# Two-expert MoE: expert results meet in a half-sum array and are scattered to the outputs, in place of an array by tokens read back at the end

## The chip, the cores and the metric

One Trainium2 chip, one core. The metric is the device time of one launch in microseconds; a comparison is made on the same chip, kernel against kernel. A core has TensorE (PE), VectorE (DVE), ScalarE (ACT), GpSimd (POOL) and SyncE (SP), and 16 DMA engines that all queues share.

## The reference

A layer of attention and retention on 512 prompt frames and 64 sample frames (576 tokens of 1024 float32 values), then a mixture of experts over 32 experts. The change touches only the second half, and in it how the experts' results reach the outputs:

```python
def hier_moe(hn, w_group, w_expert, w_gate, w_up, w_down):
    t = hn.reshape(-1, d)
    pg = softmax(t @ w_group);  g_sel = argmax(pg);  p_sel = pg[g_sel]
    el_sel = (t @ w_expert).reshape(-1, N_GROUPS, EXPERTS_PER_GROUP)[g_sel]
    top_p, top_i = top_k(softmax(el_sel), 2)
    w = p_sel * top_p / sum(top_p)
    eid = g_sel * EXPERTS_PER_GROUP + top_i        # two experts, of one group
    for e in range(32):
        a = silu(t @ w_gate[e]) * (t @ w_up[e])
        out = out + comb[:, e] * (a @ w_down[e])
...
x = x + hier_moe(rmsnorm(x, norm2_g), ...)
```

N_GROUPS is 4, EXPERTS_PER_GROUP is 8, an expert has 256 hidden units. Both experts of a token lie in one group of eight. Every token is computed by two experts, so 1152 rows in all.

## The kernel before, in words

The first part (projections, attention, retention, output projection, router logits) runs by a list of steps that `plan()` writes; it isn't touched but for one place: SP writes zeros over `y_d`, a DRAM array with two rows of 1024 for each token, by nine 512 KB transfers (line 744).

**The pairs.** The 32 experts are taken two at a time, as 16 pairs. A pair holds up to 64 rows of each of its two experts in the 128 partitions. Its weights are 6 MB (gate, up and down of two experts, 1 MB each), which SP streams from DRAM into a ring of 18 units of 1 MB, three pairs ahead at most (lines 786 to 809). For pair p:

- POOL gathers the tokens' hidden rows from `hn_d` into a row buffer `xg(p)` by an indirect transfer (`gather`, line 920). There are five row buffers (`XROWS`), so `gather(p)` waits for the scatter of pair p-5; it also waits for PE's transposes of pair p-4.
- PE transposes them (line 1272), DVE scales them into `xgT` (line 2174), PE does gate and up (line 1278), ACT the sigmoid (line 1680), DVE the product (lines 2211, 2214), PE transposes it (line 1286), DVE copies it (line 2228) and PE does down (line 1293).
- DVE adds: `ride` (line 2248) writes over the row buffer either hidden row plus y, where this is the token's first expert (flag 1 in `rides`), or y alone. POOL scatters the buffer to `y_d` (`scatter`, line 930): first expert's rows to the lower half, second expert's to the upper.

A row of the 128 that holds no token has an index beyond the bound, and nothing is moved for it. POOL runs its queue in program order:

```python
for p in range(LAST - 1):
    if p + 4 < NPAIR:
        gather(p + 4)
    scatter(p)
```

So `gather(p + 4)` waits until the scatter of pair p-1 has landed, and `scatter(p)` stands behind that. PE runs ahead: transposes of pair p+1, activation transposes of p-1, gate and up of p, down of p-1. Down of a pair waits for DVE's sum of the pair before (the same PSUM banks).

**The end.** The last two pairs (14, 15) aren't scattered. Their results are split in a high and a low half (ACT line 1691, DVE line 2281) and put on the tokens' rows by one-hot matmuls (`oh_last`, `last_rows`, lines 1334 and 1335). When the scatters of pairs 0 to 13 have landed, SP reads `y_d` back, two rows for each token (line 831, ten transfers), DVE and POOL add the two (lines 2289, 975), DVE adds the one-hot sums (line 2338), and SP stores the outputs (lines 838, 840).

More than 64 rows of one expert would run a further loop (`LEVELS`); with these inputs no expert has so many and the loop isn't entered, before or after.

Of the kernel before, what the change touches and what calls it, by code (L numbers as in the profile page):

```python
# [14 lines left out]
P = 128  # L15
# [23 lines left out]
FIN_UNIT, OVER_UNIT, YTOK_UNIT, OH_UNIT = 12, 6, 6, 4  # L39
LAST = NPAIR - 1  # L40
YOUT = [16 * (NPAIR // 2 - 1)] * 2
FIN_BANKS = [4, 0, 6, 2, 4]
# [3 lines left out]
PER_LEVEL = 7  # L46
# [3 lines left out]
FAR = 2047.0  # L50

# [183 lines left out]

def constants():
# [37 lines left out]

    dest = np.stack([np.stack([tok, tok + T_TOK * k], -1) for k in range(2)], 1) - FAR
    put("dest", dest)
    put("pair_row1", np.tile(np.arange(NE) % 2 * CAP + 1, (P, 1)))
# [25 lines left out]
def stream_step(nc, consts, x_prompt, x_sample, cache_ret_state, cache_swa_k, cache_swa_v,  # L303
# [11 lines left out]
    y_d = nc.dram_tensor("y_d", [2 * T_TOK, D], F32, kind="Internal").ap()  # L315
# [9 lines left out]
    with ExitStack() as ctx:  # L325
# [122 lines left out]
        with nc.sbuf_tensor("units_ahead_oh", [P, OH_UNIT, KD * FF], F32):  # L448
            with nc.sbuf_tensor("oh_last", [P, 2, NT, P], F32R) as oh_last:
                pass  # L450
        w_moe_a = sb("w_moe_a", [P, UNITS_A, KD * FF])

        with nc.sbuf_tensor("units_ahead", [P, FIN_UNIT - UNITS_A, KD * FF], F32):
            with nc.sbuf_tensor("y_last", [P, 2, 2, D], F32R) as y_last:
                pass
# [22 lines left out]
        rides, rides_l = ssq_qk[:, 0:NPAIR], ssq_qk[:, NPAIR:2 * NPAIR]  # L478

# [17 lines left out]
        pair_wr = const("cos").rearrange("p (j c) -> p j c", c=2 * NPAIR)  # L497
        rank_k, row_k, row_l = small[:, 60:70], small[:, 70:80], small[:, 80:90]
        lvl_a, lvl_b, level0 = small[:, 130:140], small[:, 140:150], small[:, 150:151]
        pair_dst = sb("pair_dst", [P, 2 * NT, 2 * NPAIR], F32R)  # L500
        wr_k = sb("wr_k", [P, 2, NT, 2])
        idx = sb("idx", [P, 2 * NPAIR], I32)
        idx_now = sb("idx_now", [P, 2, 1], I32)
        wr = sb("wr", [P, 2, NPAIR])
        wr_now = sb("wr_now", [P, 2, 1])
        ride_now = sb("ride_now", [P, 1])
# [5 lines left out]

        def y_tok(t, k):
            n = 2 * t + k
            return units(YTOK_UNIT + n // 2, 1)[:, 0, n % 2 * D:n % 2 * D + D]
# [105 lines left out]
        y_out = [sem(f"y_out{u}") for u in range(2)]  # L621

# [13 lines left out]
        L_out = sem("L_out")  # L636
        L_step = sem("L_step")
# [15 lines left out]
        yl_hi = sem("yl_hi")  # L653
        yl_lo = sem("yl_lo")
        oh_fin = sem("oh_fin")
        fin_ps = sem("fin_ps")
        fin_out = sem("fin_out")
# [46 lines left out]
        def _(sp):  # L704
# [8 lines left out]
            def load_gu_of(p, e):  # L713
                for m, v in enumerate((gate_v, up_v)):
                    sp.dma_start(units(gu_at(p, e, m), 1)[:, 0, :], v[2 * p + e]).then_inc(gu_in[p % 4], 16)  # L715
# [5 lines left out]
            def load_dn(p):  # L721
                for e in range(2):
                    sp.dma_start(dn_at(p, e), down_v[2 * p + e]).then_inc(dn_in[p % 4], 16)  # L723
# [46 lines left out]
            sp.dma_start(units(gu_unit(3, 0), 1)[:, 0, :], gate_v[6]).then_inc(gu_in[3], 16)  # L770
            sp.wait_ge(half_used, OUT1)
            sp.dma_start(units(gu_unit(2, 1) + 1, 1)[:, 0, :], up_v[5]).then_inc(gu_in[2], 16)
            sp.dma_start(dn_at(2, 0), down_v[4]).then_inc(dn_in[2], 16)
            sp.dma_start(units(gu_unit(3, 0) + 1, 1)[:, 0, :], up_v[6]).then_inc(gu_in[3], 16)
            sp.wait_ge(acc_done, NJ)
            load_gu_of(2, 0)
            sp.dma_start(units(gu_unit(2, 1), 1)[:, 0, :], gate_v[5]).then_inc(gu_in[2], 16)
            sp.dma_start(dn_at(2, 1), down_v[5]).then_inc(dn_in[2], 16)
# [21 lines left out]
            for half, landed in enumerate((first_half, gu_in[LAST % 4])):  # L800
                ks = slice(half * 4 * FF, half * 4 * FF + 4 * FF)
                for e in range(2):
                    for m, v in enumerate((gate_v, up_v)):
                        sp.dma_start(units(gu_unit(LAST, e) + m, 1)[:, 0, ks], v[2 * LAST + e][:, ks]
                                     ).then_inc(landed, 16)
            sp.wait_ge(y_ps, LAST - 2)
            load_dn(LAST)

            sp.wait_ge(slots_ready, 1)
            n_most = sp.value_load(most_i[0:1, 0:1], min_val=0, max_val=T_TOK)  # L810
            with sp.If(n_most > CAP):
                sp.wait_ge(y_ps, NPAIR)
                with sp.Fori(1, LEVELS) as lv:
                    with sp.Fori(0, NPAIR) as p:
                        it = (lv - 1) * NPAIR + p

                        sp.wait_ge(L_y, it + 1)
                        for e in range(2):
                            for m, v in enumerate((gate_v, up_v, down_v)):
                                sp.dma_start(units(OVER_UNIT + (2 * e + m if m < 2 else 4 + e), 1)[:, 0, :],  # L820
                                             v[bass.ds(p * 2 + e, 1)].rearrange("o p n -> p (o n)")
                                             ).then_inc(L_w, 16)
                sp.wait_ge(L_done, NPAIR * (LEVELS - 1) + 1)

            for u in range(2):
                sp.wait_ge(y_out[u], YOUT[u])
            for t in range(NT):
                n = out_rows(t)
                for k in range(2):
# [1561 lines left out]
```

## Time and profile before

| | us |
|---|---|
| three runs | 564.68, 568.24, 569.65 |
| median of the runs | 568.24 |
| span of the profiled execution, first to last instruction | 563.3 |
| MoE: first pair's matmuls to the last instruction | 323 to 563.3 |
| read back of `y_d` begins (SP line 831) | 535.5 |
| last pair's down matmuls end (PE line 1322) | 546.4 |
| TensorE's mean granted clock, 1 being full | 0.953 |

The profiled execution's time outside its span isn't listed by itself; the median of the runs is 4.9 us above the span, the lowest 1.4 us. In the rows below, a time stands from the span's start. A DMA's landing is counted from the start of the instruction that issues it.

### The profile page before, as it was taken

The page shows a single profiled execution, that of the slowest core. Times are in us where ns is not written, and L with a number is a line of the kernel's source. Part 1 is how long each engine was busy: PE and PEld are TensorE (multiplying, and loading weights), DVE is VectorE, ACT ScalarE, POOL GpSimd, SP SyncE. Part 2 cuts the span into 40 slices and gives each one's busy share as a digit, 9 for nine tenths or more (in the row PEclk, how much of TensorE's full clock was granted, in tenths as well). Part 3 has the DMA queues.
Part 4 walks back from the last instruction along what each step waited for, and adds up shares of the span by engine and source line. Part 5 has one row for each costly group of instructions (what it writes and reads, how often), then busy time and mean ns, then how long its engine had stood idle before and what let it go on. Part 6 is the DMA issues. An engine that isn't in the chain of part 4 may idle for free.

```text
span 563.3 us, 7848 instructions
## 1 busy us (share of the span) xinstructions
PE 501.6 (89%) x2907; PEld 318.3 (57%) x2907; DVE 262.0 (47%) x593; ACT 131.4 (23%) x351; POOL 156.9 (28%) x279
## 2 busy tenths in 40 slices
PE   4976999899999999999994799979999869778984
PEld 4955877777777777778884654333333333333333
DVE  2859588767344565672226622322334221112535
ACT  4754343354546322232111100000000000000110
POOL 5446683042214554741104300211111220100003
PEclk9989999799999999999997699979999998889998
DMA  8440220040026832219949799999999999999997
GB/s 294 158 127 3 75 76 2 1 144 8 2 74 234 240 123 86 79 52 407 420 167 351 296 385 396 417 423 417 417 421 420 418 420 417 419 420 423 411 411 225
DMA packets 35031, 144.75 MB, mean 257 GB/s; under 512 B 5842, under 2 KB 8994, under 8 KB 23216
## 3 DMA queue, kind: packets, MB, share of 16 engines
q1 hardware_dynamic: 26320, 129.94, 58.8%
q0 software_dynamic: 4528, 9.01, 4.3%
q10 hardware_dynamic: 4144, 5.28, 2.9%
q8 instruction: 24, 0.39, 0.3%
q14 instruction: 15, 0.12, 0.1%
HBM read 138.16 MB, written 17.30 MB: 276 GB/s over the span
## 4 chain that ended last, share of the span: by engine, by line
PE 46%; DMA 18%; DVE 13%; SPq 10%; issue 4%; ACT 3%; POOL 1%; DVEq 0%; POOLq 0%; ACTq 0%
PE banks L1051 19%; SPq L715 7%; PE banks L1278 6%; DMA w_moe_b<-in_w_up_dram 5%; DMA y_d<-rows,idx 3%; DMA y_d<-y_sb,idx 3%; SPq L723 3%; DMA w_moe_b<-y_d 3%; PE banks L1109 3%; DMA y_d<-x_row,idx 2%; PE banks L1293 2%; PE banks L1045 2%; DMA y_sb<-hn_d,idx 2%; PE banks L1194 1%; PE banks L1189 1%
## 5 line engine op out<-in xcount | busy, mean ns | idle before, releaser
L872 POOL TENSOR_TENSOR w_lo<-w_raw,w_hi 128x512 fp32r<-128x512 f32 x52 | 70.6, 1371 | 119.6 <-ACT w_hi L1556 117.7
L1278 PE MATMUL banks<-w_moe_b,xgT 128*64 128x512 f32 x224 | 67.8, 626 | 9.6 <-DMA w_moe_b<-in_w_up_dram 6.6
L1278 PE MATMUL banks<-w_moe_a,xgT 128*64 128x512 f32 x224 | 69.0, 639 | 4.9 <-DMA w_moe_a<-in_w_up_dram 4.9
L2211 DVE SCALAR_TENSOR_TENSOR glu_b<-banks,wr,glu_a 128x256 f32<-128x256 f32 x15 | 7.2, 483 | 98.4 <-ACT glu_a L1680 98.4
L1680 ACT ACTIVATE glu_a<-banks,wr 128x256 f32<-128x256 f32 x15 | 7.1, 475 | 196.6 <-PE banks L1278 183.5
L1051 PE MATMUL banks<-w_hi,xT_hi_a 128*128 128x512 f32 (+3 forms) x124 | 50.5, 408 | 1.6 <-DVE xT_lo_a L1742 1.6
L1278 PEld LDWEIGHTS banks<-w_moe_b,xgT 128*64 128x64 f32 x224 | 21.1, 144 | 48.7 <-issue 45.7
L1051 PE MATMUL banks<-w_lo,xT_hi_a 128*128 128x512 f32 (+3 forms) x124 | 48.2, 388 | 0.0
L1051 PE MATMUL banks<-w_hi,xT_lo_a 128*128 128x512 f32 (+3 forms) x124 | 48.0, 387 | 0.0
L1278 PEld LDWEIGHTS banks<-w_moe_a,xgT 128*64 128x64 f32 x224 | 21.7, 146 | 27.6 <-issue 25.8
L1051 PE MATMUL banks<-w_hi,xT_hi_b 128*128 128x512 f32 (+3 forms) x92 | 35.7, 388 | 0.8 <-issue 0.8
L1051 PE MATMUL banks<-w_lo,xT_hi_b 128*128 128x512 f32 (+3 forms) x92 | 34.0, 370 | 0.0
L1051 PE MATMUL banks<-w_hi,xT_lo_b 128*128 128x512 f32 (+3 forms) x92 | 33.9, 368 | 0.0
L1556 ACT CAST w_hi<-w_raw 128x512 fp32r<-128x512 f32 x52 | 30.7, 613 | 12.0 <-DMA w_raw<-in_w_out_dram 10.5
L1293 PE MATMUL banks<-w_moe_a,actT 128*64 128x512 f32 x144 | 32.6, 593 | 0.5 <-DVE actT L2228 0.5
L1600 ACT ACTIVATE probs<-banks,soft,rstd_qk 128x208 f32<-128x208 f32 (+1 forms) x40 | 20.6, 519 | 51.0 <-DVE soft L1922 51.0
L1051 PEld LDWEIGHTS banks<-w_hi,xT_hi_a 128*128 128x128 f32 (+1 forms) x124 | 23.8, 192 | 6.8 <-ACT xT_hi_b L1498 1.8
L1051 PEld LDWEIGHTS banks<-w_hi,xT_lo_a 128*128 128x128 f32 (+1 forms) x124 | 23.8, 192 | 5.0
L1051 PEld LDWEIGHTS banks<-w_lo,xT_hi_a 128*128 128x128 f32 (+1 forms) x124 | 23.8, 192 | 3.8
L920 POOL DMA_INDIRECT rows<-hn_d,idx x7 | 7.2, 1031 | 55.9 <-DMA y_d<-rows,idx 45.3
L2174 DVE TENSOR_TENSOR xgT<-banks,g_both 128x1024 f32<-128x1024 f32 x15 | 18.3, 1219 | 8.8 <-PE banks L1272 8.8
L1293 PEld LDWEIGHTS banks<-w_moe_a,actT 128*64 128x64 f32 x144 | 11.0, 137 | 19.9 <-issue 19.2
(334 smaller groups left out, 934.2 us busy)
## 6 DMA issues: line engine op xcount, KB each, us to landing
w_moe_a<-in_w_down_dram SPq DMA_DIRECT2D x20, 1024.0 KB, 20.3
w_moe_a<-in_w_gate_dram SPq DMA_DIRECT2D x16, 1024.0 KB, 11.6
w_moe_a<-in_w_up_dram SPq DMA_DIRECT2D x16, 1024.0 KB, 13.9
w_moe_b<-in_w_gate_dram SPq DMA_DIRECT2D x14, 1024.0 KB, 17.1
w_moe_b<-in_w_up_dram SPq DMA_DIRECT2D x14, 1024.0 KB, 17.0
w_moe_b<-in_w_down_dram SPq DMA_DIRECT2D x10, 1024.0 KB, 25.8
w_raw<-in_w_in_dram SPq DMA_DIRECT2D x34, 256.0 KB, 4.1
y_d<-in_consts_dram SPq DMA_DIRECT2D x9, 512.0 KB, 10.8
```

The source lines that it names most:

```text
L715: sp.dma_start(units(gu_at(p, e, m), 1)[:, 0, :], v[2 * p + e]).then_inc(gu_in[p % 4], 16)
L723: sp.dma_start(dn_at(p, e), down_v[2 * p + e]).then_inc(dn_in[p % 4], 16)
L872: nc.gpsimd.tensor_tensor(w_lo[:, s, :], w_raw[:, s, :], w_hi[:, s, :].bitcast(F32), ALU.subtract).then_inc(split, 1)
L920: pool.indirect_dma_start(out=xg(p), out_offset=None, in_=hn_d, in_offset=bass.IndirectOffsetOnAxis(ap=idx[:, p:p + 1], axis=0), bounds_ch ...
L1045: l = mm(into, a_hi[:, P * t:P * t + P], w, start=(kk == 0 and q == 0), stop=(kk == KD - 1 and q == 1))
L1051: l = mm(into[0:R, 0:width], a, w, start=(kk == 0 and q == 0), stop=(kk == KD - 1 and q == 2))
L1109: l = mm(sideA[64 * c2:64 * c2 + 64, b, 256 * hl + dst:256 * hl + dst + n], sqT[gs, ORDER.index(t) % DEEP, 2 * hh + hl, CH * c2:CH * c2 + CH],
L1278: l = mm(acc[64 * e:64 * e + 64, u, :].rearrange("p (m f) -> p m f", m=2), xgT[:, xu, k, 64 * e:64 * e + 64], units(at_e[e], 2)[:, :, k * ...
L1293: l = mm(acc[64 * e:64 * e + 64, 2 + n, :], actT[:, j, 64 * e:64 * e + 64], mats[e][:, j * D + n * 512:j * D + n * 512 + 512], start=(j == ...
L1556: nc.scalar.copy(w_hi[:, s, :], w_raw[:, s, :]).then_inc(hi_done, 1)
L1600: af(probs[0:R, q, hl, :], sideA[0:R, b, 256 * hl:256 * hl + KEYS], ACT.Exp, scale=rstd_qk[0:R, h + hl:h + hl + 1], bias=soft[0:R, q, 2 + ...
L2174: tt(xgT[:, u], at[:, 0:2, :].rearrange("p b (j n) -> p (b j) n", j=4), g2T.unsqueeze(2).to_broadcast([P, KD, P]), ALU.mult).then_inc(xg_e ...
```

## The change

**Order of experts.** Pair p no longer holds experts 2p and 2p+1 but two experts of different groups: even pairs of groups 0 and 1, odd pairs of groups 2 and 3. So a token stands at most once in a pair, its two pairs are both even or both odd, and one of them comes first.

**Where rows go.** `y_d` is gone, and with it its zeros, the read back, the one-hot matmuls of the last two pairs and the stores. A new array `half_d` has one row for each token (five zero transfers, four of 512 KB and one of 256 KB). In pair p a token's first expert row is scattered to `half_d` as hidden row plus y. A token's second expert's pair gathers the half sum over the row in the row buffer (`halves_back`), adds y and scatters to the outputs. Each pair thus has one plain add on DVE (`sums_of`), which waits for that gather, and, from pair 2 on, three scatters with their own index lists: prompt output, sample output, `half_d`. All 16 pairs do so; `scatter(p)` and the gathers wait for all three.

**Index lists.** The router's DVE work gets a third column: is this the token's second pair (`later`, worked out from the ranks before the table of weights is built), and seven small instructions that make the four index lists from it (`rows_to_others`).

**The last pair** has its down weights loaded by column halves, and its add in two halves.

```diff
+def expert_of(p, e):
+    return EPG * (2 * (p % 2) + e) + p // 2
...
+def landed_of(p):
+    return 16 + 48 * (p // 2)
...
-            for i in range(2 * T_TOK // P):
-                sp.dma_start(y_d[P * i:P * i + P, :], consts[:, NCONST:NCONST + D]).then_inc(y_zero, 16)
+            for t in range(NT):
+                n = out_rows(t)
+                sp.dma_start(half_d[P * t:P * t + n, :], consts[0:n, NCONST:NCONST + D]).then_inc(half_zero, 16)
...
-            for t in range(NT):
-                n = out_rows(t)
-                for k in range(2):
-                    row0 = k * T_TOK + P * t
-                    sp.dma_start(y_tok(t, k)[0:n, :], y_d[row0:row0 + n, :]).then_inc(yg_in[t], 16)
...
+            def halves_back(p):
+                pool.wait_ge(xg_ps, p + 1)
+                pool.wait_ge(y_out[p % 2], landed_of(p - 2))
+                c = column_of(p)
+                half_of(xg(p), idx[:, 2, c:c + 1], half_in[p % 2])
             def scatter(p):
-                u = p % 2
-                pool.wait_ge(y_ev, p + 1)
+                pool.wait_ge(y_ev, p + 1 if p < LAST else p + 2)
                 if p >= 2:
-                    pool.wait_ge(y_out[u], p // 2 * 16)
-                pool.indirect_dma_start(out=y_d, out_offset=bass.IndirectOffsetOnAxis(
...
+                    pool.wait_ge(y_out[p % 2], landed_of(p - 2))
+                c = column_of(p)
+                of, to = xg(p), [idx[:, k, c:c + 1] for k in range(4)]
+                if p >= 2:
+                    rows_to(y_p, SEQ, of, to[2], y_out[p % 2])
+                    rows_to(y_s, DEC, of, to[3], y_out[p % 2])
+                rows_to(half_d, T_TOK, of, to[1], y_out[p % 2])
...
-            for p in range(LAST - 1):
+            for p in range(NPAIR):
                 if p + 4 < NPAIR:
                     gather(p + 4)
+                if 0 < p < LAST:
+                    halves_back(p + 1)
                 scatter(p)
...
+            def sums_of(p):
+                dve.wait_ge(y_ps, p + 1)
+                if p >= 2:
+                    dve.wait_ge(half_in[p % 2], p // 2 * 16)
+                tt(xg(p), xg(p), acc[:, 2:4, :].rearrange("p b n -> p (b n)"), ALU.add).then_inc(y_ev, 1)
```

POOL's queue, before, in the middle of the pairs (the gather of a later pair, then the scatter of a pair; `rows`, `x_row` and `y_sb` hold the five row buffers):

```order
229 L920 DMA x_row<-hn_d,idx 128x1024 [waits y_out0,xg_ps]
230 L930 DMA y_d<-y_sb,idx 1152x1024 [waits y_out1,y_ev]
231 L920 DMA y_sb<-hn_d,idx 128x1024 [waits y_out1,xg_ps]
232 L930 DMA y_d<-y_sb,idx 1152x1024 [waits y_out0,y_ev]
233 L920 DMA y_sb<-hn_d,idx 128x1024 [waits y_out0,xg_ps]
234 L930 DMA y_d<-rows,idx 1152x1024 [waits y_out1,y_ev]
```

After, the same place:

```order
233 L910 DMA x_row<-hn_d,idx 128x1024 [waits y_out0,xg_ps]
234 L916 DMA y_sb<-half_d,idx 128x1024 [waits y_out0,xg_ps]
235 L922 DMA out_dram<-y_sb,idx 512x1024 [waits y_out1,y_ev]
236 L922 DMA out_dram<-y_sb,idx 64x1024
237 L922 DMA half_d<-y_sb,idx 576x1024
238 L910 DMA y_sb<-hn_d,idx 128x1024 [waits y_out1,xg_ps]
239 L916 DMA rows<-half_d,idx 128x1024 [waits y_out1,xg_ps]
240 L922 DMA out_dram<-y_sb,idx 512x1024 [waits y_out0,y_ev]
241 L922 DMA out_dram<-y_sb,idx 64x1024
242 L922 DMA half_d<-y_sb,idx 576x1024
```

Two indirect transfers for a pair have become five, in one queue; the waits for `y_out` (a scatter landed) and `y_ev` (DVE's sum) stand where they stood, and the wait for `y_out` is now for three scatters.

DVE's queue, before, ahead of the first pair (`cst<-glu_a,wr_k` is the table of weights, `wr_k` its factors, and the two instructions behind it find a token's rank):

```order
474 L2188 TENSOR_TENSOR wr_k<-w_k,rstd 128x10 [waits dve_step]
475 L2189 TENSOR_TENSOR cst<-glu_a,wr_k 128x320 [waits dve_step]
476 L2135 TENSOR_TENSOR xgT<-oh,banks 128x320 [waits dve_step]
477 L2136 TENSOR_REDUCE small<-xgT 128x10 [waits dve_step]
478 L2135 TENSOR_TENSOR xgT<-oh,cst 128x320 [waits dve_step]
479 L2136 TENSOR_REDUCE small<-xgT 128x10 [waits dve_step]
```

After, from the same instruction:

```order
473 L2156 TENSOR_TENSOR wr_k<-w_k,rstd 128x10 [waits dve_step]
474 L2096 TENSOR_TENSOR xgT<-oh,banks 128x320 [waits dve_step]
475 L2097 TENSOR_REDUCE small<-xgT 128x10 [waits dve_step]
476 L2160 TENSOR_SCALAR later<-small 128x10 [waits dve_step]
477 L2161 SCALAR_TENSOR_TENSOR later<-later,small 128x10 [waits dve_step]
478 L2163 TENSOR_TENSOR wr_k<-later 128x5 [waits dve_step] x2
479 L2165 TENSOR_TENSOR cst<-glu_a,wr_k 128x480 [waits dve_step]
480 L2096 TENSOR_TENSOR xgT<-oh,cst 128x320 [waits dve_step]
```

The rank is now found ahead of the table, and three kinds of small instructions stand between; the table has 480 columns in place of 320.

## Rows read from the trace of the kernel before

**Rows 1.** The page: span, and the 40 slices of PE clock and DMA.
```profile
span 563.3 us, 7848 instructions
...
PEclk9989999799999999999997699979999998889998
DMA  8440220040026832219949799999999999999997
```

**Rows 2.** Busy time by stretch: us, engines, PEclk, DMA share, GB/s.
```profile
160.00:200.00 40.00, 39.61 (x311) 29.55 (x309) 19.66 (x57) 19.29 (x54) 16.54 (x40) 1.00 0.68 222
345.00:440.00 95.00, 90.46 (x430) 34.83 (x428) 27.80 (x37) 3.32 (x7) 15.19 (x15) 0.96 1.02 419
440.00:536.00 96.00, 79.12 (x354) 32.34 (x350) 26.12 (x44) 4.09 (x8) 10.08 (x10) 0.93 1.02 419
...
547.00:563.30 16.30, 8.67 (x35) 5.69 (x33) 9.63 (x9) 0.62 (x1) 4.77 (x2) 0.84 0.75 250
```

**Rows 3.** DMA queues from 345 to 535 us; q1 weights, q0 POOL transfers.
```profile
q1 hardware_dynamic: 10474, 72.11, 91.3%
q0 software_dynamic: 3599, 7.33, 10.0%
```

**Rows 4.** POOL over time: start us, us, what, [idle before <-releaser].
```profile
362.74 1.02 POOL L920 DMA_INDIRECT rows<-hn_d,idx  x1 [8.28 <-DMA y_d<-rows,idx]
364.07 1.01 POOL L930 DMA_INDIRECT y_d<-rows,idx  x1 [0.31 <-issue]
375.17 1.01 POOL L920 DMA_INDIRECT rows<-hn_d,idx  x1 [10.09 <-DMA y_d<-rows,idx]
376.48 1.02 POOL L930 DMA_INDIRECT y_d<-x_row,idx  x1 [0.30 <-issue]
...
461.93 1.01 POOL L920 DMA_INDIRECT y_sb<-hn_d,idx  x1 [10.22 <-DMA y_d<-y_sb,idx]
```

**Rows 5.** Chain that ended last, in order of time: start us, us, what.
```profile
353.44 8.47 DMA y_d<-rows,idx
...
364.07 10.28 DMA y_d<-rows,idx
...
376.48 11.12 DMA y_d<-x_row,idx
...
400.68 9.10 DMA y_sb<-hn_d,idx
...
411.29 7.02 PE banks L1278 x32
418.30 3.43 PE banks L1293 x16
...
527.13 8.31 DMA y_d<-y_sb,idx
```

**Rows 6.** Landings of the three gathers issued from 316.8 to 319.5 us.
```profile
DMA to landing us min/median/max: 4.0/4.1/4.8
```

**Rows 7.** DVE ahead of the first pair: rank, row and weight tables.
```profile
318.21 0.53 DVE L2189 TENSOR_TENSOR cst<-glu_a,wr_k 128x320 f32<-128x320 f32 x1
318.88 0.49 DVE L2135 TENSOR_TENSOR xgT<-oh,banks 128x320 f32<-128x320 f32 x1
319.41 0.49 DVE L2136 TENSOR_REDUCE small<-xgT 128x10 f32<-128x320 f32 x1
```

**Rows 8.** PE and ACT in the last pair: start us, us, what.
```profile
539.82 0.47 ACT L1680 ACTIVATE glu_a<-banks,small 128x256 f32<-128x256 f32 x1 [7.98 <-PE banks L1434]
...
542.76 3.65 PE L1322 MATMUL banks<-w_moe_a,actT 128*64 128x512 f32 x16
...
546.46 0.75 DVE L2276 SCALAR_TENSOR_TENSOR rows<-rows,ssq_qk,banks 128x512 f32<-128x512 f32 x1 [0.81 <-PE banks L1322]
```

**Rows 9.** PE waits over the whole span: us in total, times, longest.
```profile
PE banks L1278 <- DMA w_moe_a<-in_w_up_dram: 7.8, 3, 3.5
...
PE banks L1278 <- DMA w_moe_b<-in_w_up_dram: 6.6, 2, 4.5
```

More of the change, by code:

```diff
@@ L45 @@
 LEVELS = T_TOK // CAP
[L46 removed]
+PER_LEVEL = 14
 EPS = 1e-6
@@ L621, in stream_step @@
         y_out = [sem(f"y_out{u}") for u in range(2)]
+        half_in = [sem(f"half_in{u}") for u in range(2)]
+        to_ready = sem("to_ready")
+        half_zero = sem("half_zero")
+        last_half = sem("last_half")
         L_idx = sem("L_idx")
@@ L1392, in _ @@
             act_T_of(LAST - 1)
-            down_last(0)
+            down_of(LAST - 1)
+            pe.wait_ge(xg_ev, NPAIR)
+            for k in range(KD):
+                if k == 0:
+                    pe.wait_ge(first_half, first_half_in)
+                if k == KD // 2:
+                    pe.wait_ge(gu_in[LAST % 4], LAST // 4 * 64 + 64)
+                for e in range(2):
+                    l = mm(acc[64 * e:64 * e + 64, LAST % 2, :].rearrange("p (m f) -> p m f", m=2),
+                           xgT[:, LAST % 2, k, 64 * e:64 * e + 64], units(gu_unit(LAST, e), 2)[:, :, k * FF:k * FF + FF],
+                           start=(k == 0), stop=(k == KD - 1))
+            l.then_inc(gu_ps, 1)
+            act_T_of(LAST)
+            pe.wait_ge(aT_ev, NPAIR)
+            pe.wait_ge(y_ev, LAST)
+            for n in range(2):
+                if n == 0:
+                    pe.wait_ge(last_half, 32)
+                else:
+                    pe.wait_ge(dn_in[LAST % 4], LAST // 4 * 32 + 32)
+                for j in range(2):
+                    for e in range(2):
+                        l = mm(acc[64 * e:64 * e + 64, 2 + n, :], actT[:, j, 64 * e:64 * e + 64],
+                               dn_at(LAST, e)[:, j * D + n * 512:j * D + n * 512 + 512], start=(j == 0), stop=(j == 1))
+                l.then_inc(y_ps, 1)
             pe.wait_ge(slots_ready, 1)
@@ L2188, in _ @@
             step(tt(wr_k[:, :, :, 1], w_k[:, :, :], rstd2[:, :].unsqueeze(1).to_broadcast([P, 2, NT]), ALU.mult))
-            step(tt(pair_wr[:, :, :].rearrange("p j (c a) -> p j c a", c=2),
+            pick(rank_k[:, :], ps_rank, pick_tmp)
+            whole, place = later[:, :, :].rearrange("p k t -> p (k t)"), small[:, 110:120]
+            step(ts(whole, rank_k[:, :], 0.5 - CAP / 2, TO_CAP, ALU.add, ALU.add))
+            step(stt(out=whole, in0=whole, scalar=-TO_CAP, in1=place, op0=ALU.add, op1=ALU.add))
+            for k in range(2):
+                step(tt(wr_k[:, k, :, 2], later[:, 1 - k], later[:, k], ALU.is_lt))
+            by_kind = [P, 2 * NT, 3, NPAIR]
+            step(tt(pair_wr[:, :, :].rearrange("p j (c a) -> p j c a", c=3),
                     o2_sum.unsqueeze(2).to_broadcast(by_kind),
```

338 lines of the change are left out of this document (114 added, 224 removed).

## The prediction

> **What bounds the kernel now.** I read the page's slices first. The reader sees the DMA line at 9 from the 24th slice to the last but one, while TensorE's clock line stays near full [rows 1]. By stretches, the 16 DMA engines are busy all of 345 to 536 us at 419 GB/s, with POOL issuing only 15 + 10 things there [rows 2]. So from 345 us on the weight stream sets the pace: 6 MB a pair (6 x 1.049 MB) at 419 GB/s is 15.0 us. PE waits for weights only 14.4 us in five places [rows 9], as it starts three pairs ahead. Then comes a tail: y is read back, summed and stored, and the DMA engines fall to 0.75 [rows 2].
>
> The next view is POOL's own queue. Here a gather never starts before the scatter ahead of it has landed: the idle time before it is 8 to 10 us "<-DMA y_d" [rows 4]. From the gather at 375.17 to that at 461.93 seven rounds pass, 12.4 us each. The chain that ended last runs through just these landings up to 409.8 us [rows 5]. POOL's round is thus the second bound, 12.4 us against 15.0. Only 2.6 us of slack stand between them, and the change puts three more transfers into that round.
>
> **What one indirect transfer costs.** Three prices, all counted from the start of the issue:
> - Without load, gathers issued 1.3 us apart land 4.0 to 4.8 us after their issue [rows 6]; they don't hold each other up.
> - Under the weight stream, one with nothing of POOL's ahead of it lands after 8.47, 9.10 and 8.31 us: 8.6 [rows 5].
> - The scatter issued 1.3 us behind a gather lands after 10.28 and 11.12 us, so 11.6 and 12.4 us after the gather's start (362.74, 375.17) [rows 4, 5], and seven rounds of 12.4 less 0.8 say 11.6. The second in the queue adds 11.8 - 8.6 = 3.2 us.
>
> Why 3.2, though it carries only 0.3 MB? From 345 to 535 us queue q0 moved 3599 packets [rows 3] for 25 transfers [rows 2]: 144 each, 128 for rows and 16 for the semaphore. But 7.33 MB are 1790 rows of 4 KB, 72 a transfer. So a row that holds no token still takes a packet. An engine has 9 of a transfer's 144 packets. If each takes its turn with an 8 KB weight packet (8192 B at 419/16 GB/s: 0.31 us), that is 2.8 us, and 4.5 real rows at 0.16 us make 3.5. The measured 3.2 is near it. This matters here: splitting one scatter into three by destination doesn't split its cost.
>
> [...]
>
> **The change part by part.**
>
> *Router, start of the pairs.* Ahead of the table of weights now stand the rank's two instructions (0.49 us each, 1.05 with gaps), four small ones (0.2 each from the nearest, estimated: 0.8), and a table of 480 for 320 columns (0.53 us, + 0.25) [rows 7]; the flags and half of the destination table go (-0.4). The first pair starts some 1.7 us later, at least 1.0, as PE may be a little late already. The seven index instructions run beside the first pairs' matmuls: POOL needs them only at 353 us. I cost them at nothing; without that cover they would be 1.4 us.
>
> *Zeros.* 2.4 MB fewer are written around 175 us, where the DMA engines are at 0.68 and PE is busy 39.6 of 40 us [rows 2]. PE hides it: nothing, and at most the 6 us that its bytes take.
>
> *POOL's round.* Before: gather, scatter. After, from pair 2 on: gather, half gather, three scatters, and the next round waits for the last of the three. All five carry about 180 rows (72 + 36 + 72), not 5 x 72. Under full load a round takes 0.8 (landing to next issue: 361.91 to 362.74 [rows 4, 5]) + 8.6 + 4 x 3.2 - 180/16 x 0.156 = 20.5 us. Without load it takes 0.8 + 4 x 1.32 + 4.1 = 10.2 us. Weights take 15.0 of every round; as 20.5 is over that, the stream must pause and the load falls. With the load as the share 15/T: T = 10.2 + (20.5 - 10.2) x 15/T, which gives T = 18.5 us. Bounds of the one disputed price, a further transfer under load: 1.3 us (its issue alone, [rows 4]; below that it can't go) and 3.9 (the dearer reading, 12.4 - 8.5). I take 3.2, measured for just such a transfer.
>
> Who waits behind? The gather of pair p+4, then PE's transposes of it; and DVE's `sums_of`, which now waits for the half gather and has `xgT` and `actT` behind it. Pair 2's sum (ready at 368 before) waits for a half gather issued at 366 until some 377. DVE's waits are inside POOL's round and cost nothing more by my sum.
>
> *Bytes.* 576 rows are fetched once more. q0's share of 10.0% of 190 us is 19 us for 1790 rows [rows 3]: 0.0106 us a row, 6.1 us. While rounds and not bytes set the end, that is free.
>
> *The tail.* Gone are the read back, the one-hot matmuls, adds and stores: from the last down's end at 546.4 (542.76 + 3.65) to 563.3, 16.9 us. In their place: half an add 0.75 [rows 8], 0.4 to POOL, two issues of 1.32 and a landing of 4.1 to 4.8: 8.4 us. By itself this gains 8.5 us, the change's own gain.
>
> **Sum, on the profiled span.** `gather(5)` goes out at 362.74 + 1.7 = 364.4. Its round has three transfers: 8.6 + 2 x 3.2 - 0.6 (few half rows yet) + 0.8 = 15.2, so `gather(6)` at 379.6. Nine rounds of 18.5 to `gather(15)`: 546.1. From there one path is left: landing 8.4; transposes 1.1; activation transposes 0.3; gate and up of 14 7.0; down of 13 3.5 [rows 5]; its sum 1.6; down of 14 3.5; gate and up of 15 7.0; sigmoid to down 2.9 (539.82 to 542.76) and down 3.65 [rows 8]; add, scatter and landing 8.4. That is 47.4, so the end is at 593.5. (POOL's own four short rounds, 0.8 + 3 x 1.32 + 4.6 = 9.4 each, end at 583.7, just before.) Against 563.3 that is + 30. The median of the runs stands 4.9 above the span: 598 us. At the cheap end, a further transfer at 2.2 us: full round 16.5, T 16.1, `gather(6)` 2 us sooner, end 570 + 5 = 575. At the dear end, 3.9: T 20.0, 608 + 5 = 613. TensorE's clock shows 0.93 in the stretch where PE waits most [rows 2]; with longer waits matmuls may run partly at the lower level. In the rounds that is covered by POOL; in the last path it may cost 2 to 4 us, inside the range.
>
> **Rivals.**
> - *The extra transfers overlap, and weights stay the bound: no change.* Mechanism: each of the three is worth only its issue. A full round is 0.8 + 8.6 + 4 x 1.32 = 14.7 us, just under 15.0. Then the end is 546.4 + 1.7 + 6.1 (rows) + 8.4 = 562.6, or 567. [...] It decides as soon as a further transfer costs under some 1.4 us. For it: without load transfers do overlap [rows 6]. Against: under load they don't [rows 5].
> - *As before, and the rows' bytes and the late start are hidden too: faster.* 546.4 + 8.4 = 554.8, or 560. Against: no free DMA time from 345 to 536 [rows 2].
> - *The load doesn't fall.* Rounds stay at 20.5: 379.6 + 184.5 + 47.4 = 611.5, or 616. For it: SP keeps up to three pairs ordered ahead. Against: 15.0 of weights in 20.5 leave 5.5 us empty.
> - *The change doesn't do what it says:* should the half gathers carry whole pairs, each has 72 rows; + 0.35 a round, 3 us.
>
> **How the numbers follow.** Forecast 0.74, with its dear end and the full load 0.15 more, all slower. No change 0.06, faster 0.05. A measurement of this kernel tells about 1% from no change. Faster by over 1% 0.05, within 1% 0.06, slower 0.89. The range runs from 575, the cheap end of the one price, to 616, the full load; about 0.1 is left below and 0.08 above.
>
> **What would show it.** Right: gathers on POOL 17 to 21 us apart in mid-stream; the third scatter landing over 12 us after the first one's issue; DMA slices of 7 to 8 in place of 9; PE waiting for `hn_d` gathers, and DVE's sums for `half_d`; about 8 us from the last down to the end. Wrong: rounds under 15 us with DMA slices at 9 throughout, or a stretch before 320 us that moved.

## The result, and the profile after

The changed kernel takes 614.58 us (median of 4 runs, 612.03 to 614.66), the kernel before 567.75 (564.68 to 569.65) on the same chip: ratio 1.083, 95% interval 1.080 to 1.086. The forecast was 598 us, range 575 to 616, slower with 0.89. The profiled execution took 614.49 us, its span 612.2. The direction and the mechanism (too many transfers between two waits for a landing) were right; the size was 30 us where 47 came.

The page's head and slices, against [rows 1]:

```profile
span 612.2 us, 7816 instructions
...
PEclk9998999989999999999959997969878977898897
DMA  9340300210252222498589999999798889869620
...
q1 hardware_dynamic: 24512, 120.50, 50.6%
q0 software_dynamic: 10864, 12.06, 6.0%
```

The row of nines in the DMA line now ends at the 28th slice, then 6s to 9s alternate, and it trails off over the last three. By stretches (length, busy time of PE, PEld, DVE, ACT, POOL, then PEclk, DMA share, GB/s), against [rows 2]:

```profile
345.00:440.00 95.00, 74.49 (x334) 28.92 (x332) 21.24 (x29) 2.37 (x5) 19.11 (x19) 0.87 0.99 404
440.00:540.00 100.00, 69.05 (x286) 27.59 (x284) 18.28 (x25) 2.37 (x5) 25.10 (x25) 0.83 0.88 350
540.00:580.00 40.00, 31.71 (x146) 11.82 (x142) 8.28 (x12) 1.42 (x3) 15.03 (x15) 0.87 0.75 271
580.00:612.00 32.00, 16.93 (x70) 5.41 (x68) 5.54 (x8) 0.47 (x1) 9.87 (x10) 0.84 0.16 48
```

350 GB/s where 419 flowed before. POOL's timeline shows why, one whole round (the same columns as [rows 4]):

```profile
422.44 1.03 POOL L910 DMA_INDIRECT y_sb<-hn_d,idx  x1 [15.62 <-DMA half_d<-y_sb,idx]
423.78 1.01 POOL L916 DMA_INDIRECT rows<-half_d,idx  x1 [0.31 <-issue]
425.10 1.02 POOL L922 DMA_INDIRECT out_dram<-y_sb,idx  x1 [0.30 <-issue]
426.42 0.98 POOL L922 DMA_INDIRECT out_dram<-y_sb,idx  x1 [0.30 <-issue]
427.71 0.98 POOL L922 DMA_INDIRECT half_d<-y_sb,idx  x1 [0.30 <-issue]
441.83 1.03 POOL L910 DMA_INDIRECT y_sb<-hn_d,idx  x1 [13.15 <-DMA half_d<-y_sb,idx]
```

Five transfers go out within 6.3 us, then POOL stands 13 us until the last has landed. From `gather(6)` at 380.62 to `gather(15)` at 558.30 nine rounds take 177.7 us, 19.7 each; the eight from `gather(6)` to `gather(14)` at 542.98 take 20.3 each, against 12.6 before by the same mean (375.17 to 475.65). In what follows "the round" is this mean over `gather(6)` to `gather(14)`.

From 356 to 578 us the chain that ended last now runs through nothing but these landings and the issues between them, against [rows 5]:

```profile
447.11 13.55 DMA half_d<-rows,idx
463.14 1.02 issue
464.16 1.02 POOL out_dram L922
465.49 0.99 POOL out_dram L922
466.78 14.81 DMA half_d<-rows,idx
```

So a round of 20.3 us is 0.9 from a landing to the next issue, 5.2 from the first issue to the fifth, and a landing of 14.2 on average (13.3 to 15.8). Before it was 0.8, 1.3 and 10.4. Of the 7.7 us more, about half is POOL's three further issues and half the longer landing behind them.

And who waits (waits of the span's second half: us in total, times, longest), against [rows 9]:

```profile
DVE y_sb L2229 <- DMA y_sb<-half_d,idx: 39.8, 4, 12.6
DVE rows L2229 <- DMA rows<-half_d,idx: 38.9, 4, 12.3
...
PE banks L1280 <- DMA rows<-hn_d,idx: 23.9, 5, 7.7
PE banks L1280 <- DMA y_sb<-hn_d,idx: 21.0, 4, 7.7
PE banks L1280 <- DMA x_row<-hn_d,idx: 14.4, 2, 8.2
```

PE no longer waits for weights but 59.3 us, in eleven places, for its gathered rows. DVE's waits for half sums are long and stand beside those. These are signs that the prediction named. One that it named failed: about 8 us from the last down to the end, where 11.9 passed.

### The profile page after: what moved, and what is told of

The parts are those of the page before. It is cut to its first block, busy times and chain, and to the rows that moved or that the text cites. A ratio compares the mean times of both kernels' runs of the same rounds, so it can differ in the third digit from the quotient of the medians.

```text
span 612.2 us, 7816 instructions
## 1 busy us (share of the span) xinstructions
PE 502.9 (82%) x2863; PEld 313.3 (51%) x2863; DVE 248.9 (41%) x579; ACT 128.3 (21%) x347; POOL 195.1 (32%) x321
## 3 DMA queue, kind: packets, MB, share of 16 engines
q0 software_dynamic: 10864, 12.06, 6.0%
## 4 chain that ended last, share of the span: by engine, by line
PE 35%; DMA 25%; DVE 14%; issue 11%; POOL 5%; ACT 3%; POOLq 1%; DVEq 0%; ACTq 0%
PE banks L1059 15%; DMA half_d<-rows,idx 11%; DMA half_d<-y_sb,idx 9%; DMA half_d<-x_row,idx 5%; POOL out_dram L922 4%; PE banks L1286 2%; PE banks L1117 2%; PE banks L1053 2%; PE banks L1202 1%; PE banks L1197 1%; PE banks L1236 1%; PE banks L1350 1%; PE banks L1160 1%; PE banks L1151 1%; DVE h_a L1772 1%
## 5 line engine op out<-in xcount | busy, mean ns | idle before, releaser
L1286 PE MATMUL banks<-w_moe_b,xgT 128*64 128x512 f32 x224 | 71.3, 650 | 0.0
L1286 PE MATMUL banks<-w_moe_a,xgT 128*64 128x512 f32 x224 | 71.2, 649 | 0.0
L1530 ACT CAST w_hi<-w_raw 128x512 fp32r<-128x512 f32 x52 | 30.7, 613 | 11.6 <-DMA w_raw<-in_w_out_dram 10.2
L1280 PE MATMUL banks<-cst,rows 128*128 128x128 f32 x48 | 10.1, 377 | 23.9 <-DMA rows<-hn_d,idx 23.9
L910 POOL DMA_INDIRECT y_sb<-hn_d,idx x6 | 6.1, 1014 | 68.4 <-DMA half_d<-y_sb,idx 57.2
L2229 DVE TENSOR_TENSOR rows<-rows,banks 128x1024 f32<-128x1024 f32 x6 | 7.3, 1221 | 49.7 <-DMA rows<-half_d,idx 38.9
L1280 PE MATMUL banks<-cst,y_sb 128*128 128x128 f32 x48 | 9.3, 354 | 21.0 <-DMA y_sb<-hn_d,idx 21.0
## 6 DMA issues: line engine op xcount, KB each, us to landing
w_moe_b<-in_w_up_dram SPq DMA_DIRECT2D x14, 1024.0 KB, 13.3
```

The lines of the kernel that those rows point to most:

```text
L910: pool.indirect_dma_start(out=xg(p), out_offset=None, in_=hn_d, in_offset=bass.IndirectOffsetOnAxis(ap=idx[:, 0, c:c + 1], axis=0), bounds ...
L1280: l = nc.tensor.transpose(into[:, k // 4, (k % 4) * P:(k % 4) * P + P], gv[:, k, :], ident)
L1286: l = mm(acc[64 * e:64 * e + 64, u, :].rearrange("p (m f) -> p m f", m=2), xgT[:, xu, k, 64 * e:64 * e + 64], units(at_e[e], 2)[:, :, k * ...
L1530: nc.scalar.copy(w_hi[:, s, :], w_raw[:, s, :]).then_inc(hi_done, 1)
```

## The experiments

Theory A: what costs is the number of indirect transfers between two landings that POOL waits for, about 3 us each, whatever they carry. Rival B: it is the bytes or the weight stream itself. Rival C: it is one special transfer, or DVE's new wait. Times are medians; where a kernel was timed once, the text says so. Ratios stand against the kernel before on the same chip, with their 95% interval. That kernel took 564.5 us on the chip of e1, e2, b1 and b3, and 566.3 to 567.8 on the others, so a difference in us between kernels of two chips can be off by some 3 us. Nor is one run exact: the changed kernel's four spread over 2.6 us, the six of e5, whose rounds hold the same transfers, over 6.8. Their profiles show rounds of 20.3 and 19.8 us, so a round's mean is good to some 0.5 us.

**e1: one scatter less.** The scatter to the sample outputs is left out (those rows are not written), and the count that is waited for with it.

```diff
-    return 16 + 48 * (p // 2)
+    return 16 + 32 * (p // 2)
...
-                    rows_to(y_s, DEC, of, to[3], y_out[p % 2])
```

> The changed kernel without the scatter to the sample output (0 to 12 real rows of 128 per pair); the sample output is left unwritten. Theory A (each transfer in POOL's queue costs a fixed turn under the weight stream, whether its rows are real or not, and the round from gather to gather is their sum): mid-stream rounds fall from 20.3 to about 17.4 us and the time by 30 us, to 585 (575 to 592). Rival B (what costs is the rows moved): 49 rows in all at 0.01 us, under 1 us, only the issue of 1.3 us a round at most: 597 to 614. Rival C (the round is DVE's wait for the half gather and the chain behind it): at most the 1.3 us issue a round, 597 to 614.

589.42 us (one run), round 18.0. 25 us go with a transfer that carries at most 12 rows of 128. A, within 5 us.

**e3: no half gather.** DVE's wait for it goes too; the half sums are not added.

```diff
-                if 0 < p < LAST:
-                    halves_back(p + 1)
...
-                if p >= 2:
-                    dve.wait_ge(half_in[p % 2], p // 2 * 16)
```

> The changed kernel without the half gathers and without DVE's wait for them; a second expert's row then carries the hidden row in place of the half sum. Theory A: one transfer less a round (with 0 to 79 real rows): rounds of 17 to 17.5 us, 583 (573 to 592). Rival C (the wait for the half gather is what holds the chain): rounds fall further, to the weights' 16.6 or POOL's own 17, and DVE's waits vanish; told apart from A only by a time under 573.

585.69 us (one run), round 17.9. A gather with its rows and with the wait of DVE is worth what an almost empty scatter is worth, 29 us against 25. If DVE's wait cost something of its own, it would show on top of the transfer's price; within the few us to which one run is good it doesn't, as forecast, and C falls.

**e2: one empty scatter more,** all of whose indices lie beyond the bound.

```diff
+                    rows_to(y_s, DEC, of, idx[:, 4, c:c + 1], y_out[p % 2])
```

> The changed kernel with one more scatter a pair from pair 2 on, all of whose 128 indices lie beyond the bound, so that it moves nothing. Theory A: rounds from 20.3 to about 23.2 us in mid-stream, 9 of them, and 1.3 us or more for the later ones: 614.5 + 32 = 646 (638 to 655). Rival B: nothing but issues, 614 to 630.

627.92 us (one run), round 20.7. A miss: the round grew by 0.4 us, not by 3. Of the 13 us more, 5.6 stand before `gather(5)` (371.19 for 365.63), 5.3 in the ten rounds to `gather(15)`, and the rest behind it. The first 5.6 are hardly the transfer's: PE's granted clock from 323 to 340 us was 0.69 in this execution (1.00 in the changed kernel's from 323 to 336), and the first added scatter comes later. The sixth transfer isn't worth the price of the third to fifth.

**b1 and b3: empty scatters in the kernel before,** one or three after each scatter to `y_d`, and nothing else of the change.

```diff
+                for _ in range(EMPTY):
+                    pool.indirect_dma_start(out=y_d, out_offset=bass.IndirectOffsetOnAxis(
+                                                ap=idx[:, 2 * NPAIR + p:2 * NPAIR + p + 1], axis=0),
...
```

> The kernel before with one empty scatter (all indices beyond the bound) behind each scatter. Theory A: POOL's round goes from 12.4 to 15.3 us, still under the 16.6 us that a pair's weights take at the rate of the profile (72.1 MB in 190 us): 568 to 577. A theory in which any further transfer costs its price at the end: + 14 x 3 = 42, 610. Rival B: 567 to 569.

> The kernel before with three empty scatters behind each scatter: five transfers a round, as in the changed kernel, but no half sums, no wait of DVE for a transfer, no second column of weights. Theory A: rounds of 20 to 21 us as in the changed kernel; gather of pair 15 near 574 us, last down near 613, tail 17 us: 630 (615 to 640). Rival C (DVE's wait for the half gather sets the round): 570 to 590, as nothing waits there.

b1: 575.05 us, ratio 1.016 (1.005 to 1.028), round 14.8. b3: 615.53 us (one run), round 19.1. Three transfers that move nothing, added to a kernel that is otherwise the old one, cost as much as the whole change (614.58); a part of it comes before the rounds (`gather(5)` at 374.95, for 362.74 before and 365.63 after), most from them. The stretches of b3 read like those of the changed kernel:

```profile
345.00:440.00 95.00, 70.99 (x316) 27.76 (x314) 22.45 (x30) 2.37 (x5) 23.81 (x24) 0.86 0.96 385
440.00:540.00 100.00, 68.68 (x298) 27.29 (x296) 18.93 (x25) 2.37 (x5) 24.82 (x25) 0.83 0.90 354
```

This shows that it isn't bytes: B falls for the round. In the round the three cost about the same, 2.3 us the first and 2.2 each of the next two, of which 1.3 each is the issue. In the kernel's time the first costs some 11 us, as the round stays under the weights' pace, and the next two 40.

**l1: little weight traffic.** From pair 4 on each weight transfer carries 128 KB in place of 1 MB (256 of a unit's 2048 columns); the rest of these weights isn't loaded.

```diff
+                    n = 256 if p >= 4 else KD * FF
+                    sp.dma_start(units(gu_at(p, e, m), 1)[:, 0, 0:n], v[expert_of(p, e)][:, 0:n]).then_inc(gu_in[p % 4], 16)
```

> The changed kernel with only the first 256 of 2048 columns of each weight transfer of pairs 4 to 14 (the rest of each unit keeps what it held), the same transfers, waits and instructions. Theory A: without the weight stream a transfer waits for no turns; rounds of five transfers fall to about 10.5 us, then PE's own 11.8 us a pair binds: 530 (520 to 545). If the round's price is on POOL or DVE itself and not in the shared DMA engines: rounds stay near 18 to 20, 590 to 614.

534.18 us (one run), round 11.9, from the third on between 11.5 and 12.0 each. The five transfers of the changed kernel take 20.3 us beside the weight stream and at most 11.9 without most of it. At most, for PE is now busy without a pause and may itself set this pace:

```profile
345.00:440.00 95.00, 94.48 (x464) 36.02 (x465) 29.73 (x42) 3.78 (x8) 34.88 (x35) 1.00 0.44 119
```

POOL goes on 3.7 to 3.9 us after it issued the last one. Less the 0.8 to the next issue, that is a landing of about 3 us, under the 4.0 to 4.8 of [rows 6], which stand at much the same DMA share (0.47 from 316.8 to 321 us). And DVE's sum is now in the round:

```profile
404.23 1.03 POOL L912 DMA_INDIRECT y_sb<-hn_d,idx  x1 [2.95 <-DMA half_d<-y_sb,idx]
405.57 1.02 POOL L918 DMA_INDIRECT rows<-half_d,idx  x1 [0.31 <-issue]
409.48 1.02 POOL L924 DMA_INDIRECT out_dram<-rows,idx  x1 [2.89 <-DVE rows L2231]
410.80 0.99 POOL L924 DMA_INDIRECT out_dram<-rows,idx  x1 [0.31 <-issue]
412.10 0.97 POOL L924 DMA_INDIRECT half_d<-rows,idx  x1 [0.30 <-issue]
415.79 1.02 POOL L912 DMA_INDIRECT rows<-hn_d,idx  x1 [2.72 <-DMA half_d<-rows,idx]
```

The other half of the question is what POOL waits for. Four kernels keep all five transfers and change only that.

**e4: the half scatter first,** with a semaphore of its own, so that the output scatters are under way while POOL waits for it; `gather(p + 4)` comes last.

```diff
             for p in range(NPAIR):
-                if p + 4 < NPAIR:
-                    gather(p + 4)
+                scatter_half(p)
                 if 0 < p < LAST:
                     halves_back(p + 1)
-                scatter(p)
+                scatter_out(p)
+                if p and p + 4 < NPAIR:
+                    gather(p + 4)
```

> The changed kernel, all of its work, in another order on POOL: the scatter to the half sums goes first and has a semaphore of its own, the half gather of the next pair waits for that one only, then the two output scatters, then the gather of a later pair (a round late); the half scatters of pairs 14 and 15, which have no first rows, are left out. Theory A with its cause (the wait for the last of five transfers drains the queue once a round, 5 us of start latency and the rest in series): the queue is no longer drained, five transfers take some 15 us of turns beside 16.6 to 17.5 us of weights: 575 (567 to 590). If the turns alone (throughput) bind and not the drain: 600 to 614.

597.67 us, ratio 1.055 (1.050 to 1.060), round 17.4. Less than half of the expected gain. The gather is now the last in the queue, and PE waits 53 us for it, in seven places; in turn POOL waits for DVE's sum:

```profile
412.75 1.03 POOL L913 DMA_INDIRECT y_sb<-hn_d,idx  x1 [0.30 <-issue]
430.66 1.01 POOL L925 DMA_INDIRECT half_d<-rows,idx  x1 [16.88 <-DVE rows L2243]
```

Rounds alternate between 13 and 23 us. One wait had taken another's place.

**e8: a sixth row buffer alone,** in the input units of the weights' ring, free by then (`XROWS` 5 to 6). `gather(p+4)` then needs no landing of pair p-1; the half gather behind it still does.

```diff
-XROWS = 5
+XROWS = 6
...
-            return rows[:, b, :] if b < 2 else x_row[:, 0, :] if b == 2 else y_sb[:, b - 3, :]
+            return rows[:, b, :] if b < 2 else x_row[:, 0, :] if b == 2 else y_sb[:, b - 3, :] if b < 5 else w_moe_x[:, 0, 0:D]
```

> The changed kernel with the sixth row buffer of e6 and nothing else: the order of POOL's transfers is that of the change. gather(p+4) no longer waits for the scatters of pair p-1 and goes out right behind them, but the half gather of pair p+1 still does, as the half scatter is the last of the three. One of five transfers is then under way while POOL waits. If the wait for the last landing is what costs (and one transfer less stands in the drained part): rounds of 17 to 18 us, 588 us (580 to 597). If the buffer alone had made e6's gain: 14 us and 575 us. If only the order had made it: 20 us and 612 us.

585.58 us, ratio 1.032 (1.027 to 1.037), round 17.15: as expected, and neither the buffer alone nor the order alone is the whole. The gather now stands ahead of the long wait:

```profile
417.12 0.97 POOL L922 DMA_INDIRECT half_d<-y_sb,idx  x1 [0.30 <-issue]
418.40 1.03 POOL L910 DMA_INDIRECT y_sb<-hn_d,idx  x1 [0.30 <-issue]
431.21 1.01 POOL L916 DMA_INDIRECT rows<-half_d,idx  x1 [11.79 <-DMA half_d<-y_sb,idx]
```

**e6: sixth buffer and order together.** For pair p: half gather of p+1, half scatter of p, gather of p+4, then the two output scatters.

```diff
             for p in range(NPAIR):
-                scatter_half(p)
                 if 0 < p < LAST:
                     halves_back(p + 1)
-                scatter_out(p)
-                if p and p + 4 < NPAIR:
+                if p < 2:
                     gather(p + 4)
+                scatter_half(p)
+                if p > 1 and p + 4 < NPAIR:
+                    gather(p + 4)
+                scatter_out(p)
```

> The changed kernel with the order of e4 and a sixth buffer for gathered rows (in the wide input buffer, free by then). POOL's order for pair p: halves_back(p+1), gather(p+4), scatter_half(p), the two output scatters: the next pair's rows stand ahead of the three scatters in the queue, and no transfer of a round is waited for before the next round is issued. Theory A (what bounds is the transfers themselves, each takes its turns beside the weights' packets): five transfers still cost most of the changed kernel's 20.3 us round; only the landing that nothing covered goes, so rounds of 16.5 to 19 us, 575 to 600 us in all. Theory B (what bounds is the wait for the last scatter before the next gather, the drain of the queue): rounds fall to the weights' 15 us, 555 to 570 us. PE's waits for hn_d gathers (53 us in e4) should shrink to under 20 us by either.

575.10 us, ratio 1.013 (1.008 to 1.018): 39.5 of the 47 us are back, with the change's every transfer still there. The time is A's cheap edge and outside theory B's 555 to 570, but the round is 13.8 us, below A's 16.5 and B's 15: what I had left in was still part of the drained landing. Its stretches, and its queues from 345 to 540 us:

```profile
345.00:440.00 95.00, 82.42 (x382) 31.46 (x380) 25.55 (x35) 2.85 (x6) 29.35 (x29) 0.95 1.01 410
440.00:540.00 100.00, 85.60 (x384) 32.34 (x382) 24.91 (x34) 3.33 (x7) 30.40 (x31) 0.91 1.02 416
...
q1 hardware_dynamic: 10095, 71.29, 88.2%
q0 software_dynamic: 8454, 9.15, 13.3%
```

The DMA engines are full again throughout, and the chain that ended last goes through a weight transfer again (first line), as in the kernel before (second line):

```profile
528.24 21.06 DMA w_moe_a<-in_w_up_dram
...
486.10 28.27 DMA w_moe_b<-in_w_up_dram
```

A part of what is left against the old kernel is DMA time of POOL's queue. For the same 195 us that kernel shows

```profile
q1 hardware_dynamic: 10791, 74.20, 91.6%
q0 software_dynamic: 3600, 7.33, 9.8%
```

so q0 takes 3.5% more, 6.8 us, where the forecast had 6.1 for the second fetch of 576 rows. The 1.82 MB more are 444 rows, 4.7 us at the forecast's price of a row; the rest would be the packets without a row. Only here, where the stream sets the pace, do B's bytes count. They don't account for all: the last down ends at 562.6 for 546.4, 16 us later, and the DMA engines' share from 320 to 345 us is 0.81 for 0.94. What makes up the rest was not taken apart.

**e7: e6 with four transfers.** The sample tokens' second rows go to `half_d` too, and SP copies those 64 rows to the output at the end.

```diff
-                if p < LAST - 1:
+                if True:
                     rows_to(half_d, T_TOK, xg(p), idx[:, 1, c:c + 1], hd_out[p % 2])
...
-                    rows_to(y_s, DEC, xg(p), idx[:, 3, c:c + 1], y_out[p % 2])
...
+            sp.dma_start(y_s, half_d[SEQ:T_TOK, :]).then_inc(tail_out, 16)
```

> e6 without the scatter to the sample tokens' outputs: their second rows go to the half-sum array too and SyncE copies 64 rows of it to the output at the end, so POOL's round has four transfers and the drain is gone. By the price of 3 us a transfer: rounds of 15 us or just over, the weights' own rate; end 3 us later for the copy; 570 us (558 to 582), which is the time before the change. If rounds stay at 17 or more, each transfer costs the weight stream itself DMA time and not only POOL's round.

572.85 us, ratio 1.011 (1.007 to 1.015), round 13.2. Within what was expected, but only 2.3 us better than e6, inside the spread of its runs (570.6 to 576.2), where the same transfer was worth 25 us in e1. The stream is the bound (the chain that ended last holds a weight transfer of 21.12 us, as in e6), so a transfer off POOL's round buys little. No version that does all the work is faster than the kernel before.

**e5 and t1: the end.** After its last landing the changed kernel runs on some 5 us: SP waits 5.1 us for PE's sequencer at the last barrier. Two explanations were tried: the jump over the overflow loop (e5 takes that loop's code out on all engines; with these inputs it is never entered), and an indirect transfer as the last work (t1 adds an empty one to the end of the kernel before).

```diff
-            n_most = pe.value_load(most_i[0:1, 0:1], min_val=0, max_val=T_TOK)
-            with pe.If(n_most > CAP):
...
```

> The changed kernel without the loop for experts with over 64 rows, which these inputs never enter, and without the test for it. The profile shows SyncE waiting 5.1 us at the end for TensorE's sequencer at the last barrier, after the last landing. Theory: the jump over the loop, now at the very end, costs about 5 us there: 609 to 610. Rival (the end is the landing of the last scatters, the barrier is hidden): 614.

```diff
+            pool.wait_ge(fin_out, 16 * NT)
+            pool.indirect_dma_start(out=y_d, out_offset=bass.IndirectOffsetOnAxis(
...
+            sp.wait_ge(end_out, 16)
```

> The kernel before the change with one indirect scatter by POOL, all of whose indices are out of bounds, issued after the last output store has landed, and SyncE waiting for it. If an indirect transfer at the end costs its issue and landing only: 1.3 + 4.1 to 4.8 less overlap, so + 4 to 5 us, 572 us. If the last barrier also waits some 5 us more whenever POOL's indirect transfer is the last work (as the changed kernel's trace shows): + 9 to 10 us, 577 us.

e5: 612.41 us, ratio 1.083 (1.078 to 1.088), and SP still waits 5.4 us, so the jump is not the cause. t1: 570.26 us (one run). The transfer goes out at 564.10 and lands 2.1 us later, and then SP waits 2.0 us more for PE's sequencer, to the span's end at 568.4; the kernel before has 0.2 there. The queue's packets from 563.5 us on, the landing and SP's wait:

```profile
q0 software_dynamic: 144, 0.00, 1.3%
...
DMA to landing us min/median/max: 2.1/2.1/2.1
...
SPq L326 <- PEq L326: 2.0, 1, 2.0
```

The 4 to 5 us expected came out, but by luck: half of them is the barrier. So one indirect transfer as the last work brings some 1.8 us of wait, and not 5. Side by side, the wait grows, roughly, with how many of them POOL issues after the last sum: 2.0 us with one (t1); 3.8, 4.8 and 4.8 with two (e1, e4, e6); 4.0 to 5.4 with three (the changed kernel, e3, e5, e8, l1); 6.2 with four (e2); 0.2 where a plain transfer by SP ends the kernel (before, b1, b3, e7). No run varied that number alone, and what PE's sequencer does there stays open.

## Why the prediction was right, and where its size was off

By the number of transfers in a round, and what POOL waits for (the old order unless said):

| transfers | kernel | round, us | by the prediction's full-load sum: 0.8 + 8.6 + 3.2 (n - 1) - (72 n - rows) / 16 x 0.156 |
|---|---|---|---|
| 2 | before | 12.6 | 12.6 |
| 3 | b1 | 14.8 | 15.1 |
| 4 | e1, e3 | 18.0, 17.9 | 17.9, 17.6 |
| 5 | after | 20.3 | 20.5 |
| 5, three empty | b3 | 19.1 | 20.1 |
| 6, one empty | e2 | 20.7 | 22.9 |
| 5, little load | l1 | 11.9 | |
| 5, six buffers | e8 | 17.15 | |
| 5, six buffers and e4's split | e6 | 13.8 | |

- **A further transfer under load, 3.2 us: right** for the change's five, as the sum of 20.5 against 20.3 shows; the empty ones came to 2.2, where the sum has 2.5, inside the bounds. At six the price falls away (e2), which the sum doesn't give; why is open. Its count of packets was right too: of q0's 10864, 74 transfers of 144 make 10656. An empty transfer alone has 144, all under 512 B (t1, 563.5 to 569 us). The split in 128 and 16 agrees with the copy that ends e7: 32 packets (q1, 568 to 572 us), 16 of them under 512 B; and a transfer adds 16 to its semaphore (`landed_of`), which leaves 128 of the 144 for the rows, real or not. Of the 14083 packets of all queues from 345 to 535 us in the kernel before, 8305 have 8 KB or more: the weights'. Nine packets an engine is a mean, 144 by 16, and that each waits one turn behind a weight packet was the author's estimate; no run shows the turns one by one.
- **"Splitting one scatter into three by destination doesn't split its cost": right,** shown by b3, where three transfers with no rows give 615.5 us, and cost 6.6 us a round where their issues alone make 4.0.
- **Start of the pairs, + 1.7: right.** `gather(5)` stands at 365.63 for 364.4; the first part before it, which the change doesn't touch, was itself 1.6 us later in this execution (a POOL memset at 300.64 for 299.00), and from the factors `wr_k` to DVE's first `xgT` the router now takes 5.86 us for 4.20 (319.40 to 325.26, 318.00 to 322.20 before), 1.66 more. The three-transfer round took 15.0 us for 15.2.
- **The step that failed: "the stream must pause and the load falls", T = 10.2 + (20.5 - 10.2) x 15/T = 18.5.** Measured 20.3, which is the full-load value; over nine rounds 177.7 us for 166.5, + 11.2. The rival "the load doesn't fall" had the time, 616, and got only 0.15. Two things were wrong. First, the average stands in for the load at the moment of the transfers. The stretches of one round (482.45 to 502.07) show that the pause falls behind them:

```profile
482.45:486.00 3.55, 2.09 (x10) 0.42 (x6) 0.22 (x1) 0.00 (x0) 2.94 (x3) 1.00 0.89 362
486.00:490.00 4.00, 0.00 (x0) 0.00 (x0) 0.00 (x0) 0.00 (x0) 2.08 (x3) 0.88 1.02 423
490.00:494.00 4.00, 3.40 (x14) 2.49 (x16) 0.30 (x1) 0.00 (x0) 0.00 (x0) 0.50 1.01 408
494.00:498.00 4.00, 4.00 (x18) 1.20 (x16) 2.38 (x3) 0.00 (x0) 0.00 (x0) 0.76 1.03 399
498.00:502.07 4.07, 4.07 (x22) 1.26 (x18) 0.06 (x1) 0.47 (x1) 0.00 (x0) 1.00 0.42 168
```

  SP orders the next six megabytes at 481.15 to 485.4, released by PE, whose gate and up end at 481.1 and down at 484.5, which frees units of the ring. POOL issues its five transfers at 482.45 to 488.7, released by the landing at 481.60. Two releasers, but they come within 1.5 us of each other in this round and in those beside it (orders at 460.96, 501.50, 521.96; gathers at 461.51, 502.07, 523.24). That PE starts each pair at the landing of a round's first transfer would explain it; no run separates the two. The DMA share is 0.89 in the first stretch, full until 498, and falls to 0.42 only in the last 4 us, when most of the transfers have had their load. Second, "15.0 us a pair" divides a pair's 6.29 MB by the rate of both queues. The weights alone moved 72.11 MB in 190 us [rows 3], 16.6 us a pair; with that the same formula gives 19.1. So 0.6 us of the miss of 1.8 is this slip, and the rest, by this reading, the average.
- **Last path, 47.4 us: measured 53.9 (558.30 to 612.2), + 6.5.** Three terms. Gate and up of 14 took 8.33 us for 7.0 and the last down 5.26 for 3.65, as the granted clock was low over a part of each. In the round above it was 0.50 from 490 to 494, after PE's idle 484.5 to 490.6, then 0.76 to 498 and 1.00 only from there. Here, in the same columns, it was 0.50 before gate and up of 14 begin and over their first 2.6 us (568.4 to 571), 0.85 over the whole of them, and 0.69 over the last down:

```profile
563.00:568.40 5.40, 2.26 (x10) 2.00 (x10) 0.40 (x1) 0.00 (x0) 1.23 (x2) 0.50 1.02 383
568.44:577.00 8.56, 8.56 (x35) 2.73 (x36) 2.25 (x3) 0.17 (x1) 3.97 (x4) 0.85 0.73 261
...
595.00:600.30 5.30, 5.26 (x16) 1.43 (x16) 0.69 (x1) 0.00 (x0) 0.00 (x0) 0.69 0.01 3
```

  That is + 2.9 us, which the text had named as 2 to 4 but not put in the sum. From the last down's end to the span's end 11.9 us for 8.4: + 3.5. In it are the 5.1 us of the barrier, not foreseen, while the last scatter, with few rows and no load, lands at most 2.7 us after its issue (604.37 to 607.1) for 4.6. The rest is near 0.
- **Outside the span, 4.9: 2.3** in the profiled execution, - 2.6. The 4.9 set the median of one group of runs against the span of another execution; in each execution of the kernel before for which both are on record the two are 1.7 to 1.9 apart. Sum: 1.0 + 11.2 + 6.5 - 2.6 is 16.1, so 598 + 16.1 = 614.1, against 614.49 of that execution.
- **The tail's own gain, 8.5: measured 16.9 - 11.9 = 5.0.**
- **The half gathers, at nothing: right** (e3). **Bytes, free while rounds set the end: right,** and 6.8 us once they don't (e6).
- **The rival "overlap, no change": fell in this order of work, but e6 comes close to it** (573.0 for its 562.6 as a span): its 562.6 was to be the end, and is where the last down ends and the last add begins; add, landings and barrier then take 10.4. That the two numbers meet is chance: the rival's overlap was of the transfers alone, and e6 needed another order and another buffer. The forecast saw a bound in the count of transfers alone. e8 and e6 show that a round is count plus one uncovered landing: 29.0 us of 47 went with one gather ahead of the wait, 10.5 more with the split. That the first transfer's 8.6 could be covered by a sixth buffer was not looked at.

## What to carry to other kernels

Count indirect transfers between two waits for a landing, not their rows: beside a full weight stream each further one up to the fifth cost 2.2 to 3.2 us of the round here (2.6 on average for the change's three), the empty ones 2.2. Before taking the share of a busy resource as the load on something else, look when in the round each of them runs, for the transfers here met the full load though the average was 0.88. And if a queue is waited empty once in a loop, one more buffer that lets the next gather go out ahead of the wait is worth as much (29 us here) as the best of the transfers taken out (29 and 25).

## What was not expected of the hardware

- A scatter whose 128 indices all lie beyond the bound costs a round under load 2.3 us (b1) and, three of them, 6.6 us (b3, 19.1 for 12.6); the sixth transfer of a round only 0.4 (e2). Each is still 144 packets of next to no bytes, as t1's row shows.
- In l1 the same five transfers take 11.9 us a round at a DMA share of 0.44 (345 to 440 us), with PE never idle, so the weight stream makes up at least 8.4 of the changed kernel's 20.3 us.
- The last barrier waits 3.8 to 6.2 us for PE's sequencer when two to four of POOL's scatters end the kernel, and 2.0 when one does (t1), though PE's last matmul is 9 to 14 us past in the former; the jump over unused code doesn't explain it. e7, whose end is a copy by SP, waits 0.2 and ends at 572.0, 9.7 us behind the start of its last add at 562.3.
